# Two of the three modulation blocks of a one-core transformer step: weighted and added on GpSimd, summed over the partitions once a block on TensorE

## The reference, cut to what matters

```python
c_act = silu(c)                                   # 1 x 1024
mod = c_act @ w_ada + b_ada                       # 1 x 6144
shift_m, scale_m, gate_m, shift_f, scale_f, gate_f = split(mod, 6)
h = rms_norm(x, g) * (1 + scale_m) + shift_m
p = h @ w_in                                      # 256 x 5632: u_f, v, b_g, c_g, two gates
z = gate_a * (fourier_mix(u_f) @ w_fourier) + gate_b * ((b_g * conv3(c_g * v)) @ w_conv_out)
x = x + gate_m * (z @ w_o)
h2 = rms_norm(x, g2) * (1 + scale_f) + shift_f
x = x + gate_f * expert_choice_moe(h2, ...)       # 16 experts, 32 rows each, three weights of 8 MB each
...                                               # then the second block and a last norm
```

## Time and profile before

| | us |
|---|---|
| median of 3 runs | 1370.62 (1369.79 to 1371.24) |
| profiled execution, its time | 1372.34 |
| profiled execution, its span | 1370.3 |
| TensorE busy | 1010.5 |
| VectorE busy | 339.4 |
| ScalarE busy | 247.2 |
| GpSimd busy | 24.4 |
| HBM read | 494.64 MB |

### The profile page before, as it was taken

The page is one execution under the profiler, slowest core; times in us unless marked ns, Lnnn a source line. Parts: engine busy times, 40 slices in busy tenths (PEclk is TensorE's granted clock), DMA queues, the critical chain, the costliest instruction groups (busy, mean ns, idle before and its releaser), DMA issues.

```text
span 1370.3 us, 15755 instructions
## 1 busy us (share of the span) xinstructions
PE 1010.5 (74%) x6816; PEld 522.4 (38%) x6817; DVE 339.4 (25%) x492; ACT 247.2 (18%) x355; POOL 24.4 (2%) x80
## 2 busy tenths in 40 slices
PE   4899999796756756676575666666566665899998
PEld 1778999621111111111111111111111111599978
DVE  0645356520000000000000000000000000577855
ACT  1423334200000000000000000000000000457735
POOL 2000000000000000000000000000000000000000
PEclk8899999898788798877878878877898988999999
DMA  9997796889999999999999999999999999964340
GB/s 333 374 336 265 237 298 230 359 360 427 429 427 427 428 428 429 428 429 429 429 428 429 429 429 429 429 429 429 429 429 429 428 428 426 322 238 154 105 142 32
DMA packets 89609, 496.38 MB, mean 362 GB/s; under 512 B 5160, under 2 KB 57804, under 8 KB 61148
## 3 DMA queue, kind: packets, MB, share of 16 engines
q1 hardware_dynamic: 87888, 490.36, 88.3%
q0 software_dynamic: 1296, 5.19, 1.1%
q10 hardware_dynamic: 380, 0.16, 0.0%
HBM read 494.64 MB, written 1.05 MB: 362 GB/s over the span
## 4 chain that ended last, share of the span: by engine, by line
DMA 60%; PE 36%; DVE 2%; issue 1%; ACT 0%; SPq 0%; ACTq 0%
DMA ring<-in_w_down_e 21%; DMA ring<-in_w_gate_e 18%; DMA ring<-in_w_up_e 18%; PE psum L608 8%; PE psum L610 7%; PE psum L609 7%; PE psum L883 4%; PE psum L909 2%; DMA ring<-in_w_ada 2%; PE psum L674 1%; DMA ring<-in_w_in 1%; PE psum L946 1%; PE psum L1030 1%; PE psum L729 1%; PE psum L979 1%
## 5 line engine op out<-in xcount | busy, mean ns | idle before, releaser
L883 PE MATMUL psum<-ring,arena 128*32 128x512 f32 x2048 | 302.1, 721 | 195.7 <-DMA ring<-in_w_up_e 117.2
L909 PE MATMUL psum<-ring,arena 128*32 128x512 f32 x992 | 175.7, 826 | 97.5 <-DMA ring<-in_w_down_e 90.1
L883 PEld LDWEIGHTS psum<-ring,arena 128*32 128x32 f32 x2048 | 60.5, 121 | 395.0 <-DMA ring<-in_w_up_e 158.2
L1425 DVE TENSOR_TENSOR ring_r<-ring,ring_r 128x2048 fp32r<-128x2048 f32 x55 | 124.6, 2287 | 65.5 <-ACT ring_r L1108 65.4
L909 PEld LDWEIGHTS psum<-ring,arena 128*32 128x32 f32 x992 | 36.1, 132 | 220.1 <-DMA ring<-in_w_down_e 157.6
L608 PE MATMUL psum<-ring_r,ht_hi 128*128 128x256 f32 (+1 forms) x384 | 114.5, 298 | 5.2 <-DVE ht_lo L1429 5.2
L1108 ACT ACTIVATE ring_r<-ring 128x2048 fp32r<-128x2048 f32 x55 | 103.9, 1911 | 57.9 <-PE psum L610 31.1
L610 PE MATMUL psum<-ring_r,ht_lo 128*128 128x256 f32 (+1 forms) x384 | 113.3, 295 | 0.0
L609 PE MATMUL psum<-ring_r,ht_hi 128*128 128x256 f32 (+1 forms) x384 | 112.9, 294 | 0.0
L1219 ACT ACTIVATE arena<-psum 128x512 f32<-128x512 f32 x16 | 9.6, 597 | 547.8 <-PE psum L883 547.8
L608 PE MATMUL psum<-ht_hi,ring_r 128*128 128x256 f32 x384 | 108.1, 281 | 0.0
(11 more groups left out here) (258 smaller groups left out, 762.6 us busy)
## 6 DMA issues: line engine op xcount, KB each, us to landing
ring<-in_w_gate_e SPq DMA_DIRECT2D x64, 2048.0 KB, 36.3
ring<-in_w_up_e SPq DMA_DIRECT2D x64, 2048.0 KB, 35.8
ring<-in_w_down_e SPq DMA_DIRECT2D x58, 2048.0 KB, 35.9
ring<-in_w_in SPq DMA_DIRECT2D x38, 1024.0 KB, 10.1
ring<-in_w_ada SPq DMA_DIRECT2D x24, 1024.0 KB, 11.0
ring<-in_w_down_e SPq DMA_DIRECT2D x8, 1024.0 KB, 22.6
ring<-in_w_conv_out SPq DMA_DIRECT2D x4, 1024.0 KB, 5.9
ring<-in_w_o SPq DMA_DIRECT2D x4, 1024.0 KB, 11.2
```

The costliest lines, as they stand in the source:

```text
L883: last = mm(psum[32 * g:32 * g + 32, b, :], cur[h][:, k, :], w[:, g, :], start=(k == 0), stop=(k == KD - 1), tile_position=(0, 32 * g))
L909: last = mm(psum[32 * q:32 * q + 32, 2 + n, :], act_t[:, f % 4, (f // 4) * CAP:(f // 4 + 1) * CAP], w[:, kk, n * BANK:(n + 1) * BANK], sta ...
L1425: V.tensor_tensor(ring_r[place(s)][:], ring[:, place(s), :], ring_r[part_place[s]][:].bitcast(F32), ALU.subtract).then_inc(lo_ready, 1)
```

## The change

GpSimd multiplies each slot of blocks 1 and 2 by its c_act column (in place; for k = 0 into a place of its own, `ada_sum`) and adds it into `ada_sum`. TensorE waits for each step at the place where it had its products, and sums `ada_sum` over the partitions after the eighth step, with four products of the same shape with ones. The slot is counted as used together with the first slot of the next unit that has slots. `ada_sum` takes one of the four part places, so that three are left, and pair 6 waits for the third w_o slot. ScalarE waits for the partition sums. (Declarations of the semaphores and of `ada_sum = ring[:, SUM_PLACE, :]` are left out.)

```diff
-HEAD_PARTS, HEAD_RING = 4, RING - 4
+HEAD_PARTS, HEAD_RING = 3, RING - 4
+SUM_PLACE, HEAD_PART_ROOM = RING - 4, RING - 3
...
-        part_place = {s: HEAD_RING + n % HEAD_PARTS for n, s in enumerate(head_split)}
+        part_place = {s: HEAD_PART_ROOM + n % HEAD_PARTS for n, s in enumerate(head_split)}
...
+        ada_step = {bk: n + 1 for n, bk in enumerate(bk for u in sorted(ADA_BEFORE) for bk in ADA_BEFORE[u])}
+
+        def ada_before(u):
+
+            since = max((v for v in range(u) if HEAD_UNITS[v][1]), default=-1)
+            return sum(len(ADA_BEFORE.get(v, ())) for v in range(since + 1, u + 1))
...
-            for used, d in ((2, 4), (2, 6), (4, 5), (4, 7)):
+            for used, d in ((2, 4), (3, 6), (4, 5), (4, 7)):
...
+            pool.wait_ge(c_ready, 1)
+            for (b, k), step in ada_step.items():
+                s = first_slot[f"ada{b}_{k}"]
+                arrived(pool, s)
+                if k == 0:
+                    if b == 2:
+                        pool.wait_ge(ada_summed, 1)
+                    nc.gpsimd.tensor_scalar(ada_sum, ring[:, place(s), :], c_act[:, k:k + 1], None, ALU.mult).then_inc(ada_done, 1)
+                else:
+                    w = ring[:, place(s), :]
+                    nc.gpsimd.tensor_scalar(w, w, c_act[:, k:k + 1], None, ALU.mult).then_inc(ada_weighted, 1)
+                    pool.wait_ge(ada_weighted, step - b)
+                    pool.wait_ge(ada_done, step - 1)
+                    nc.gpsimd.tensor_tensor(ada_sum, w, ada_sum, ALU.add).then_inc(ada_done, 1)
+
             await_bank(pool, "head", head_u["ya1"], 1)
...
-            def transposed_product(s, u, act_parts):
+            def transposed_product(s, u, act_parts, others=0):
...
-                    last.then_inc(slot_used, 1)
+                    last.then_inc(slot_used, 1 if j else 1 + others)
...
-            def modulation(b, k, to):
-
-                s = first_slot[f"ada{b}_{k}"]
+            def sum_partitions(b, to):
+
+                for g in range(4):
+                    last = mm(psum[32 * g:32 * g + 32, to, :], ones[:, 0:32], shaped(ada_sum, g=4, n=512)[:, g, :], start=True, stop=True,
+                              tile_position=(0, 32 * g))
+                last.then_inc(ada_summed, 1)
+
+            def modulation(k, to):
+
+                s = first_slot[f"ada0_{k}"]
...
-                for bk in ADA_BEFORE.get(u, ()):
-                    if bk == (1, 0):
-                        pe.wait_ge(mod_ready, 1)
-                    modulation(*bk, 3 + bk[0])
+                for b, k in ADA_BEFORE.get(u, ()):
+                    pe.wait_ge(ada_done, ada_step[b, k])
+                    if k == KD - 1:
+                        if b == 1:
+                            pe.wait_ge(mod_ready, 1)
+                        sum_partitions(b, 3 + b)
...
-                    transposed_product(first_slot[name], u, (ht_hi, ht_lo))
+                    transposed_product(first_slot[name], u, (ht_hi, ht_lo), ada_before(u))
...
-                act.wait_ge(slot_used, first_slot[f"ada{b}_{KD - 1}"] + 1)
+                if b:
+                    act.wait_ge(ada_summed, b)
+                else:
+                    act.wait_ge(slot_used, first_slot[f"ada0_{KD - 1}"] + 1)
```

More of the change, by code:

```diff
@@ L199, in build @@
         mod_rows = [area(5640, BANK), area(1536, BANK), area(2048, BANK)]
+        ada_sum = ring[:, SUM_PLACE, :]
         dfts = shaped(gfin, t=TT, n=2 * SEQ)
@@ L272, in build @@
         gate_row_done, gate_row_ready = sem("gate_row_done"), sem("gate_row_ready")
+        ada_weighted, ada_done, ada_summed = sem("ada_slots_weighted"), sem("ada_slots_added"), sem("ada_partitions_summed")
         squared, mean_ready, root_ready, scale_ready, xr_ready = (sem(n) for n in ("squared", "mean_ready", "root_ready", "scale_ready", "xr_ready"))
@@ L701, in _ @@
                     nc.tensor.transpose(psum[:, 6, 0:5 + KD], vec2[0:5 + KD, :], ident[0:5 + KD, 0:5 + KD]).then_inc(gain_turned, 1)
-                modulation(0, k, 4)
+                modulation(k, 4)
             turn_modulation(0, 5)
             for u, (name, slots) in enumerate(HEAD_UNITS):
-                for bk in ADA_BEFORE.get(u, ()):
-                    if bk == (1, 0):
-                        pe.wait_ge(mod_ready, 1)
-                    modulation(*bk, 3 + bk[0])
+                for b, k in ADA_BEFORE.get(u, ()):
[4 more added lines that the diff above has]
+                        sum_partitions(b, 3 + b)
                 if name == "fourier_in":
@@ L748, in _ @@
                                                      (fm_hi[:, k, :], fm_lo[:, k, :]), k == 0, k == FG - 1)
-                        end_first(last) if j == 0 else end_second(last, slots)
+                        end_first(last) if j == 0 else end_second(last, slots + ada_before(u))
                 else:
                     pe.wait_ge(st_ready, 4)
-                    transposed_product(first_slot[name], u, (st_hi, st_lo))
+                    transposed_product(first_slot[name], u, (st_hi, st_lo), ada_before(u))
                     if name == "yb0":
```

## The result

The changed kernel takes 1428.34 us (median of 4 runs, 1426.14 to 1430.83) against 1370.93 (4 runs) for the kernel before beside it: ratio 1.0415, interval 1.0403 to 1.0428. It is 57.4 us slower, where 1375.6 was forecast. The profiled execution has a span of 1424.3 us, 54.0 more than before.

A forecast was written before the change was run, and what follows sets the result against it. The expert stage is bound by its DMA bytes, its start by TensorE's chain through head and routing. Terms -13.9 + 4.1 + 14.8 = +5.0 on the 1370.6 median gave 1375.6 us, range 1359.5 to 1388.

The forecast's parts named there:

- The removal, 13.9 us: Head, TensorE: sixteen modulation steps go and two partition sums come, 0.99 us each, so 13.9 us less on the chain.
- Release of the slots: Ada slots released 5.7 us later, 10 where a unit without slots lies between; the queue's lead covers it, cost nothing.
- pair 6: Expert pair d=6 waits for the third w_o slot instead of the second; other pairs keep the engines busy, cost nothing.
- the places: Three places for high parts make ScalarE's copy wait for product n-3, not n-4; hidden except at the fourth w_o slot.
- The last split, 4.1 us: Fourth w_o slot's split comes later, delaying VectorE's gate rows and router shift, so TensorE waits 4.1 us at L809.
- GpSimd's work: Head: multiply 2.0 us, add 4.4 us, 6.6 us a slot with the wait; alone, GpSimd is in time everywhere.
- The third rival: GpSimd slower by itself: add of 6.1 us gives 1396, multiply as dear as the add 1407; chance 0.14.
- If the two can't read together, their times add.: GpSimd's 81.0 us and VectorE's 52.2 us from 51.7 end at 184.9 against 170.1: 14.8 us late at step 14.
- The sum: Whole kernel: -13.9 for the removal, +4.1 for the last split, +14.8 for taking turns, +5.0 us in all.
- The expert stage: Stretch from 285 us on stays unchanged but for its start, since it lasts as long as its bytes.

The follow-up runs named there:

- The version on VectorE: Kernel before, each slot's multiply and add as one VectorE instruction instead of TensorE's steps, one ada slot moved, gate rows ahead of the last split: 1357.69 us, ratio 0.9894.
- with the gate rows first: VectorE's gate rows and router shift put ahead of its fourth w_o split: kernel before with three high-part places 1371.60 us; changed kernel 1425.12 us.
- 6.2 alone: Kernel before with three places for high parts instead of four and pair 6 behind the third w_o slot, nothing on GpSimd: 1377.26 us, ratio 1.0045.
- with nobody waiting for GpSimd: Kernel before with three places, TensorE keeping its modulation steps, GpSimd doing multiplies and adds on the spare place: 1416.14 us, ratio 1.033.
- the short copies: Changed kernel with GpSimd's multiplies replaced by copies of the same place, leaving out the c_act weights: 1401.33 us, ratio 1.0222.
- memsets: Changed kernel with GpSimd's multiply and add replaced by three memsets each, leaving out the modulation of both blocks: 1392.30 us, ratio 1.016.

## Why the prediction was wrong, point by point

**The removal, 13.9 us.** Right. The version on VectorE gets 13.6 of it.

**Release of the slots, pair 6, the places.** Nothing, and right: with the gate rows first three places and pair 6 cost nothing, and in the version on VectorE, which releases the slots as late, TensorE waits for no arrival from 41 to 240 us.

**The last split, 4.1 us.** Right in its mechanism (the wait was 4.4), mis-sized: 6.2 alone; within the change 3.2, which isn't clear of 6.2 by these runs.

**GpSimd's work: "13 multiplies at 2.0 (26.0)".** The first step that failed. I costed the multiply as a copy, because both read one operand. It takes 5.45 us. The third rival named it ("a multiply as dear as the add gives 13 x 2.4 = 31, 1407"), at 0.14 with a dearer add. The add, taken at 4.4, was right (4.49); the figure of 4497 ns in the Trainium skill (GPSIMD Engine Reference, Elementwise — side-by-side cycle accounting) agrees with that.

**"If the two can't read together, their times add."** The second step that failed, in its size. In kind it held: reads hold each other up (38.9 us with nobody waiting for GpSimd), writes leave the two-input instructions alone. The rule of the Trainium skill (SBUF — State Buffer, Who interferes with whom) says just this, and that a tensor_scalar can take the shared ports by itself; the 1834 ns of the one-input taps beside memsets agree. "For the whole instruction", as the prediction has it, holds here for the adds; a multiply lets two-input taps pass in its last 1.45 us. What I summed wrongly was VectorE's side: I entered the taps at 6.7 + 2.3, as if two queues were laid end to end. But while GpSimd has the next instruction ready, VectorE gets only the openings, and a tap of 0.35 us takes 3.3 to 5.5. The taps took 70.8 us, and 51.9 with the short copies. I asked which of GpSimd's steps is late; the late one was VectorE, with TensorE waiting 50.6 us for it and 8.1 for GpSimd.

**The sum.** Put the measured durations into my own sum: 70.9 + 54.0 + 2.2 + 52.2 from 51.7 on end at 231.0 against 170.1, 60.9 late; -13.9 + 6.2 + 60.9 = +53.2, near the measured 57.4. That is agreement by chance. With the durations I had assumed, the same sum gives +5.0 and the chip +29.7. So of the 52.4 us between forecast and result, 2.1 come from the last split (6.2 for 4.1), 22.6 from the turns, and 27.7 from the multiply (57.4 - 29.7), where the sum would have asked 13 x 3.45 = 44.9 for it.

**The expert stage.** Right: unchanged but for its start, 55.6 us later.

Open: why a multiply of GpSimd lets the two-input taps through in its last 1.45 us and an add doesn't, and 4.6 us of the head's delay.

## What to carry to other kernels

Before elementwise work goes to an idle engine, ask which busy engine reads the same memory, and look for its shortest instructions: they lose most, up to the neighbour's whole instruction each, and not by their own length. A duration is carried over only between rows of the same operation; a copy prices no multiply. If the busy engine can do the work itself in a quarter of the time with one fused instruction, it is the better place although it is busier: here 2.35 us a slot on VectorE beat 10.2 on GpSimd, 1357.69 against 1425.12 us with the gate rows first in both.

## What the runs showed of the hardware

- On GpSimd a multiply of 128 x 1024 by a constant took 2.79 us, by a column 2.84, an add 1.89, a copy 1.04; at 2048 the multiply took 5.45, the add 4.49, a memset 1.81.
- Beside GpSimd's long instructions, a tensor_scalar of 128 x 256 on VectorE took 4.8 us for 0.35, a scalar_tensor_tensor 2.1 for 0.48, a split 3.2 for 2.3.
- Beside an add of GpSimd one instruction of VectorE passed, as the add ended; beside a multiply two-input taps passed from 1.45 us before its end on, at their full 0.48 us.
- With GpSimd's instructions cut to 256 columns the taps took 0.59 and 0.57 us, and GpSimd's pieces 1.07 and 0.99 in the mean (0.92 and 0.72 in the median).
- Beside memsets only the one-input tensor_scalar was held up (1834 ns).
